# A chunked RWKV scan in two directions: each engine gets an order of its own for the steps

## What is computed

```python
def step(s, inp):
    w_t, k_t, v_t, kk_t, a_t = inp[:5]
    sa = jnp.einsum('bhvk,bhk->bhv', s, kk_t)
    s = (s * w_t[:, :, None, :] - sa[..., None] * (kk_t * a_t)[:, :, None, :]
         + v_t[..., None] * k_t[:, :, None, :])
    if not want_out:
        return s, None
    return s, jnp.einsum('bhvk,bhk->bhv', s, inp[5])
```

## Time and profile before

| what | us |
|---|---|
| median of 3 runs (2244.3 to 2248.84) | 2245.53 |
| the profiled execution, its own time | 2250.13 |
| its span | 2248.3 |
| the scan in it, first VectorE `prepare` at 978.70 to last `b_y` at 1285.61 | 306.91 |

### The profile page before, as it was taken

How to read it: one execution, slowest core, us unless ns; L and a number is a source line. 1 busy time by engine, 2 the same in 40 slices (tenths; PEclk the granted TensorE clock), 3 DMA queues, 4 the chain that set the end, 5 groups by cost and what they waited for, 6 DMA issues and landing times. The chain is left out here.

```text
span 2248.3 us, 37355 instructions
## 1 busy us (share of the span) xinstructions
PE 2052.2 (91%) x16083; PEld 1694.8 (75%) x16083; DVE 1360.4 (61%) x1287; ACT 803.0 (36%) x874; POOL 278.6 (12%) x135
## 2 busy tenths in 40 slices
PE   7679999999899989966777799989999999999997
PEld 3258888888688876656667688778888888888886
DVE  3465666665438547768877678466565656554444
ACT  1231112113062225534444365344343434333333
POOL 0242213123104214401000020000000000000000
PEclk9689999999899999989898999999999999999999
DMA  9989888886264378986444087545555555555553
GB/s 324 349 273 330 309 311 299 311 317 192 90 170 106 85 192 269 304 203 171 85 85 83 34 194 251 219 133 185 188 187 192 187 193 186 192 188 195 197 188 112
DMA packets 406658, 454.08 MB, mean 202 GB/s; under 512 B 108062, under 2 KB 357262, under 8 KB 389246
## 3 DMA queue, kind: packets, MB, share of 16 engines
q1 hardware_dynamic: 398912, 441.04, 62.1%
q10 hardware_dynamic: 7614, 11.10, 1.3%
HBM read 413.89 MB, written 38.22 MB: 201 GB/s over the span
## 5 line engine op out<-in xcount | busy, mean ns | idle before, releaser
L215 DVE TENSOR_TENSOR f_w_lo<-t_w_raw,f_w_hi 128x2048 fp32r<-128x2048 f32 x132 | 302.3, 2290 | 307.0 <-ACT f_w_hi L209 307.0
L270 PE MATMUL pf<-h,f_w_hi 128*128 128x512 f32 x1320 | 463.9, 395 | 0.0
L209 ACT ACTIVATE f_w_hi<-t_w_raw 128x2048 fp32r<-128x2048 f32 x132 | 253.2, 1918 | 446.6 <-PE pf L270 284.4
L269 PE MATMUL pf<-h,f_w_lo 128*128 128x256 f32 x1320 | 367.4, 278 | 0.3 <-DVE h L2606 0.3
L270 PEld LDWEIGHTS pf<-h,f_w_hi 128*128 128x128 f32 x1320 | 247.6, 188 | 54.3
L269 PEld LDWEIGHTS pf<-h,f_w_lo 128*128 128x128 f32 x1320 | 248.3, 188 | 4.6 <-DVE h L2606 0.6
L209 ACT ACTIVATE p_w_hi<-h_w_raw 128x2048 fp32r<-128x2048 f32 (+1 forms) x52 | 96.4, 1902 | 340.3 <-DVE stage L726 252.1
L261 PE MATMUL p_in<-h,p_w_lo 128*128 128x512 f32 (+1 forms) x512 | 199.3, 389 | 0.0
L259 PE MATMUL p_in<-h,p_w_hi 128*128 128x512 f32 (+1 forms) x512 | 199.3, 389 | 0.0
L260 PE MATMUL p_in<-h,p_w_hi 128*128 128x512 f32 (+1 forms) x512 | 199.2, 389 | 0.0
L858 DVE SCALAR_TENSOR_TENSOR late_acc<-h_of_x,siluc,late_acc 128x2048 f32<-128x2048 f32 x60 | 159.7, 2662 | 39.7 <-DMA h_of_x<-in_ada_w 38.2
(11 more groups left out here) (403 smaller groups left out, 3344.2 us busy)
## 6 DMA issues: line engine op xcount, KB each, us to landing
h_of_x<-in_ada_w SPq DMA_DIRECT2D x64, 1024.0 KB, 5.2
h_w_raw<-in_w_in SPq DMA_DIRECT2D x51, 1024.0 KB, 7.5
t_w_raw<-in_ffn_w_gate SPq DMA_DIRECT2D x44, 1024.0 KB, 5.1
t_w_raw<-in_ffn_w_up SPq DMA_DIRECT2D x44, 1024.0 KB, 5.1
t_w_raw<-in_ffn_w_down SPq DMA_DIRECT2D x44, 1024.0 KB, 4.9
h_w_raw<-in_ada_w SPq DMA_DIRECT2D x32, 1024.0 KB, 8.8
gate_w<-in_w_in SPq DMA_DIRECT2D x32, 1024.0 KB, 5.9
t_w_raw<-in_w_out SPq DMA_DIRECT2D x16, 1024.0 KB, 5.9
```

The source lines that it names most:

```text
L209: act.activation(self.hi[:, m % self.S, 0:w], self.raw[:, s, 0:w], ACT.Copy)\
L215: eng.tensor_tensor(self.lo[:, m % self.S, 0:w], self.raw[:, s, 0:w], b32(self.hi[:, m % self.S, 0:w]), ALU.subtract)\
L269: pe.matmul(hi, wl, x[:, 0, k, :], start=False, stop=False)
L270: return pe.matmul(both, wh, x[:, :, k, :], start=False, stop=last)
```

## The change

`run` goes, and each of the three engines gets a list of its own (`run_vector`, `run_scalar`, `run_tensor`). In a list, `every`, `context` and `latents` say for which kind of item the line holds, and the number behind the step's name says how many rounds the item lies back; a fourth is the level. The instructions themselves, their sizes, tiles and semaphores are the same; two waits are touched so that the orders are allowed. The lists of VectorE and TensorE in full:

```diff
-        def run(step):
...
+        def calls(step, n):
+
+            def call(kinds, name, back, *which):
+                if 0 <= n - back < len(HALVES) and latent(HALVES[n - back][0]) in kinds:
+                    step[name](*HALVES[n - back], *which)
+
+            def every(*at):
+                call((False, True), *at)
...
+                def run_vector(step):
+                    for n in range(-1, len(HALVES) + 3):
+                        every, context, latents = calls(step, n)
+                        every("prepare2", 1)
+                        context("stage", 2, 2)
+                        every("prepare", 0)
+                        latents("stage", 2, 2)
+                        latents("output", 3)
+                        latents("prepare3", 1)
+                        context("stage", 2, 3)
+                        every("state", 3)
+                        latents("stage", 2, 3)
+                        latents("scores1", 1)
+                        every("stage", 2, 4)
+                        latents("scores2", 1)
+                        latents("scores3", 1)
+                        latents("close", 2)
+                        context("scores1", 1)
+                        context("scores2", 1)
+                        context("open", 1)
+                        context("close", 2)
+                        latents("open", 1)
+                        every("prepare1", 0)
+                        context("stage", 1, 1)
+                        every("halve", 2)
+                        latents("stage", 1, 1)
...
                 def scores3(c, d):
-                    pe.wait_ge(sm("first", d), c + 1)
                     if not latent(c):
                         return
+                    pe.wait_ge(sm("first", d), c + 1)
...
                 def tokens(c, d):
                     pe.wait_ge(sm("in_kkv", d), c * 16 + 16)
+                    pe.wait_ge(sm("first", d), c + 1)
...
+                def run_tensor(step):
+                    for n in range(-1, len(HALVES) + 3):
+                        every, context, latents = calls(step, n)
+                        latents("output", 2)
+                        latents("state", 2)
+                        latents("grow", 1, 2)
+                        latents("scores1", 0)
+                        latents("scores2", 0)
+                        every("grow", 1, 3)
+                        latents("scores3", 0)
+                        context("scores1", 0)
+                        context("scores2", 0)
+                        every("grow", 1, 4)
+                        latents("own_part", 1)
+                        context("tokens", 0)
+                        context("flips", 0)
+                        context("own_part", 1)
+                        context("grow", 0, 0)
+                        latents("tokens", 0)
+                        latents("flips", 0)
+                        every("inverse", 1)
+                        every("rhs", 1)
+                        latents("grow", 0, 0)
+                        latents("u", 1)
+                        context("grow", 0, 1)
+                        context("u", 1)
+                        latents("from_state", 1)
+                        context("grow", 0, 2)
+                        latents("grow", 0, 1)
+                        context("state", 1)
```

More of the change, by code:

```diff
@@ L1403, in phase_rwkv_scan, with context, latents @@
+        def calls(step, n):
[4 more added lines that the diff above has]
+                call((False, True), *at)
+            def context(*at):
+                call((False,), *at)
+            def latents(*at):
+                call((True,), *at)
+            return every, context, latents
         with nc.Block() as block:
@@ L1550, in output @@
                     dve.tensor_tensor(by_parity(yat), by_parity(yat), narrow(pb[d]), ALU.add).then_inc(sm("ysum", d), 1)
-                run(dict(prepare=prepare, prepare1=prepare1, prepare2=prepare2, prepare3=prepare3, stage=stage, scores1=scores1, scores2=scores2, scores3=scores3,
+                def run_vector(step):
[24 more added lines that the diff above has]
+                        latents("stage", 1, 1)
+                run_vector(dict(prepare=prepare, prepare1=prepare1, prepare2=prepare2, prepare3=prepare3, stage=stage, scores1=scores1, scores2=scores2, scores3=scores3,
                          close=close, open=open_, halve=halve, state=state, output=output))
@@ L1614, in u_step, with run_scalar @@
                         act.activation(own_blocks(uv[d], b)[HEAD[b]], narrow(pa[d])[HEAD[b]], ACT.Copy).then_inc(sm("uc", d), 1)
-                run(dict(prepare=prepare, forward=forward, ends=ends, output=output,
+                def run_scalar(step):
+                    for n in range(-1, len(HALVES) + 3):
+                        every, context, latents = calls(step, n)
+                        latents("u", 2)
+                        context("stage", 1, 3)
+                        context("prepare", -1)
+                        latents("stage", 1, 2)
+                        latents("output", 2)
+                        latents("stage", 1, 3)
+                        context("forward", -1)
+                        latents("prepare", -1)
+                        context("stage", 1, 4)
+                        latents("forward", -1)
+                        context("close", 1)
+                        latents("stage", 1, 4)
+                        latents("close", 1)
+                        every("tokens", 0)
+                        context("flips", 0)
+                        context("ends", 0)
+                        latents("flips", 0)
+                        context("stage", 0, 1)
+                        context("rhs", 1)
+                        context("stage", 0, 2)
+                        latents("rhs", 1)
+                        latents("ends", 0)
+                        latents("stage", 0, 1)
+                        context("u", 1)
+                run_scalar(dict(prepare=prepare, forward=forward, ends=ends, output=output,
                          tokens=tokens, flips=flips, stage=stage, close=close, rhs=rhs_copy, u=u_step))
@@ L1781, in state @@
                     last.then_inc(sm("st", d), 1)
-                run(dict(scores1=scores1, scores2=scores2, tokens=tokens, flips=flips, scores3=scores3,
+                def run_tensor(step):
+                    for n in range(-1, len(HALVES) + 3):
+                        every, context, latents = calls(step, n)
+                        latents("output", 2)
+                        latents("state", 2)
[9 more added lines that the diff above has]
+                        context("tokens", 0)
+                        context("flips", 0)
+                        context("own_part", 1)
+                        context("grow", 0, 0)
+                        latents("tokens", 0)
+                        latents("flips", 0)
+                        every("inverse", 1)
[3 more added lines that the diff above has]
+                        context("grow", 0, 1)
+                        context("u", 1)
+                        latents("from_state", 1)
+                        context("grow", 0, 2)
+                        latents("grow", 0, 1)
+                        context("state", 1)
+                run_tensor(dict(scores1=scores1, scores2=scores2, tokens=tokens, flips=flips, scores3=scores3,
                          grow=grow, inverse=inverse, own_part=own_part, rhs=rhs_sum, u=u_step,
```

## The result

The changed kernel takes 2232.28 us in the median of 5 runs (2222.72 to 2235.86), the kernel before 2245.53 (2244.3 to 2248.84): a ratio of 0.993, with a 95% interval of 0.9907 to 0.9952. It is faster by 13 us in the medians, and by 11 to 21 in the interval; forecast were 36.4 and 2209, with 2201 to 2223. A second comparison of the same two kernels on another occasion gave 2224.06 (6 runs) against 2245.71: 0.9912, interval 0.9886 to 0.9937. Over all 14 executions the changed kernel has a mean of 2227.3 and a median of 2228.3, from 2218.4 to 2235.86; the kernel before goes from 2234.9 to 2256.46 over all its own. One execution of the kernel before (3531.01 us, at a granted clock of 0.6) and one of its form with thin loads (3445.44, at 0.56) ran in a slow state and are left out of the ratios.

The account below looks back on a forecast made before the run. VectorE was taken as the bound, its idle time the gain: context 7.1, change-over 4.1, latent 25.2, start and end 0, in all 36.4 us. From 2250.13 to 2213.7, less 4.6 to the median: 2209, range 2201 to 2223.

Parts of the forecast that it names:

- change-over: Round between the context and latent rounds: forecast 17.5 us instead of 21.63, 4.1 less.
- The base (Sum): Whole execution: the profiled 2250.13 us less 36.4 gives 2213.7; the median, 4.6 below that execution, gives 2209.
- Step (5), context rounds: Seven context rounds: waits behind `q` and ahead of `cross` go; 13.9 us for 14.61 undisturbed, 7.1 less in all.
- Step (6), disturbances: Latent rounds: 5.0 of 15.3 us lost to disturbances such as TensorE stops stay; context rounds: 8 of 10.2.
- Step (4), the state's way back: From `xt` to `S` in latent rounds: 5.2 us against about 5.0 of VectorE work, a new wait of 0.3.
- Step (1), `scores3`: Latent rounds: `scores3` issued behind `grow` 3 instead of `grow` 4, so VectorE's stall of 1.54 us goes.
- The end (Sum): Stretch behind the latent rounds, 20.25 us: a chain without cover, its change put at 0.
- its own signs: Right: latent rounds 16 to 17 us, VectorE busy over 0.93, no wait over 0.3 ahead of `r` or `stage` 1.
- the waits that come back elsewhere: Latent rounds: `cross` waits for `grow` 4 and `S` for `state`, 1 us each per round: 2237 us, chance 0.05.
- the clock falling as often as before: TensorE's clock: latent rounds keep their loss of 2.19 us each, saving 25.0 in all: 2220.5 us, chance 0.18.
- The slower rival: Loads of `s` come too late and hold VectorE, each round losing 0.7 us net: 2256 us, chance 0.04.
- a denser order that keeps the full clock: Latent part: no disturbance is left, saving 42.5 us in all: 2203 us, chance 0.15.

Follow-up runs that it names:

- thin loads: From the second chunk on `ld`, `kkv`, `rc` bring only their first unit (stale inputs): changed kernel 2213.58 us (0.9847), kernel before 2245.56 (0.9998).
- undo of `prepare1`: Changed kernel with `prepare1` (`s`) behind `stage` 1 again instead of ahead of it in latent rounds: 2225.61 us (0.9915).
- late loads: Changed kernel with loads of `s`, `kkv`, `rc` of items 10 to 15 issued only once `state` of item k-3 is done: 2222.73 us (0.9894).

## Why the prediction was wrong, by its own steps

The direction and the mechanism held: VectorE bounds the scan, most of its waits went, and the undisturbed rounds came out at 13.80 and 16.6. The size did not: 36.4 us forecast, 22.1 in the scan over seven profiles, 13 and 22 between the medians of the two comparisons. Of the 23 us by which 2209 missed 2232, some 14 lie in the scan's terms: base 5.1, context rounds 4.1, the end 2.4, disturbances 1.7, the start 0.8, change-over 0.3. The other 9 lie outside the scan.

- **The base (Sum).** This is the largest of the terms that failed. The forecast took away disturbances that stood in one profile, of an execution with a scan of 306.9 us where three average 301.8. It then took 4.6 off once more to come from that execution to the median, though those 4.6 were, by the later profiles, the same disturbances. That makes 5.1 of the 23 us.
- **Step (5), context rounds.** The undisturbed round is right, the sum is not: 109.1 to 110.2 instead of 105.3. The first round took 15.1, and two to three rounds were long with the burst of loads as before, in part because VectorE's own operations stretched beside GpSimd's; the prediction had no term for that. Besides, the first `open` came 0.8 later. The half with the new context order alone measured 0.9993: 7.1 us forecast, at most 6 by the interval. The wait of 2.6 us of `prepare` for the load of item 5 was mis-sized: it was 0.56 and 0.83 in two profiles of four and absent in the others.
- **Step (6), disturbances.** Sized at 5.0 in the latent part; the four profiles have 120.4 to 122.8, so 5.6 to 8.0 over the 114.8 of undisturbed rounds: 1.7 us off in the mean. The argument for it was half wrong. "TensorE has slack in most places" fails for the stops: their place in the stream is fixed, and in the new order it fell into `state`, where step (4) had left no cover.
- **Step (4), the state's way back.** 0.3 us undisturbed was about right (often none); under a stop it became 0.5 to 2.5. The way shares its slack with `stage` 1: the undo of `prepare1` moved the wait from the one to the other, at no cost that its times show.
- **Step (1), `scores3`.** The mechanism is right and its worth was mis-sized. Priced at 1.54 a round, some 12 us, it measured some 33 when undone alone in the new order, where the clock falls in every latent round. The gain hangs on it: without it the other parts are slower than the kernel before. Whether it alone, moved in the old common order, would give the gain was not tried.
- **The end (Sum).** The prediction put its change at 0 and so kept 20.25; it took 21.64 to 24.97 at a clock of 0.75 to 0.92, where it was 1.00 or 0.92 before: 2.4 us.
- **The rest of the miss.** The prediction had what lies outside the scan keep its length. The 9 us left over are the difference between the mean rest of the program in the profiles and in the first five timed runs; their second comparison came out 8 us lower. The rest of the program varied by 13 us between profiles (1938.5 to 1951.5) where no instruction differs. What makes it vary was not tried, so this part stays open.

By its own signs: the clock is over 0.95 in the latent stretch, as it said. But single waits of up to 0.8 us ahead of `r` stayed, VectorE is busy 0.89 to 0.90 of the latent rounds, not over 0.93, the mean round is 17.2 to 17.5, and waits ahead of `S` of over 1 us and a longer end are among the signs of being wrong.

Of the rivals, the waits that come back elsewhere (2237) are nearest to 2232, and the clock falling as often as before (2220.5) is nearest to the mean of all executions; both by luck. Waits ahead of `S` did come back, 3.3 to 5.4 us in the latent rounds, but not in every round, and the mean round is 17.4 and not 20.6. The clock falls less in the changed kernel's four profiles (0.97 to 0.99 in the latent rounds against 0.89 to 0.94). The slower rival fell: VectorE waited for no load in any latent round.

It stays open why the thin loads gave 10 us or more in time where their two scans are 0 and 6 us shorter. And the late loads removed the stops from `state` without a shorter latent part; whether the clock's falls there come with that order or with that one execution isn't settled.

## What to carry to other kernels

A saving that is an absence of disturbances needs several profiles of the kernel before: the stretch summed here varied by 11 us between executions, half of what was won. When an engine in lockstep with TensorE waits on it, price the wait with the clock that falls behind it, and put TensorE's longest product where its input is first ready, ahead of small work that waits for a chain. And where slack is spent to the last 0.3 us, look for stops of the issuing engine that come once per round at a fixed instruction: they move into the tight place.

## What the runs showed of the hardware

TensorE stopped at the same matmuls in all four profiles of the same program, some 500 matmuls apart, for 0.2 to 2.4 us each; the stops sum to 8 to 11 us in the latent rounds while the loads run beside them, to 1.1 and 1.2 with thin loads (in the old order 3.7 to 6.7 and 1.5), and to 4.3 with loads issued later. That the loads lengthen them is shown; that they are waits for the instructions themselves fits this, but was not shown.

The clock fell from 1.00 to 0.50 behind stretches of 2 us in which TensorE was busy 0.39 to 0.61 of 2.00 us, and behind a stop of 2.35 us; behind one of 1.79 us it stayed at 1.00. One such wait per round held the mean clock of 153 us at 0.81, with TensorE's records busy 124 of them. By the Trainium skill ("TensorE: Matmul & The Clock Gate", What's actually happening) the clock follows recent activity; the trace agrees with it in these falls. The rival drawn from it, a denser order that keeps the full clock, held in single rounds only.

A VectorE operation of 0.69 us took up to 4.25 beside a GpSimd instruction of 4.82.
